# Block 2 of a two-block transformer kernel: the latent values' two parts further apart, and weights behind short pieces split sooner

## The reference

```python
h = rmsnorm(x, pre_norm_mix[l])
proj = h @ w_in[l]
g_a, g_b, qa, ka, va, cq, ckv, kr = jnp.split(proj, SPLIT_IDX, axis=-1)
out_a = swa_sink_alibi_attention(qa, ka, va, positions, sinks[l])
qb = (rmsnorm(cq, q_a_norm[l]) @ w_q_b[l]).reshape(B, S, N_HEADS_B, Q_HEAD_B)
kvb = (rmsnorm(ckv, kv_a_norm[l]) @ w_kv_b[l]).reshape(B, S, N_HEADS_B, KV_HEAD_B)
...
out_b = mla_attention(q_nope, q_rope, k_nope, k_rope, v_b)
merged = jax.nn.sigmoid(g_a) * (out_a @ w_o_a[l]) + jax.nn.sigmoid(g_b) * (out_b @ w_o_b[l])
x = x + rmsnorm(merged @ w_out[l], post_norm_mix[l])
h2 = rmsnorm(x, pre_norm_mlp[l])
y = jnp.square(jax.nn.relu(h2 @ w_up[l])) @ w_down[l]
x = x + rmsnorm(y, post_norm_mlp[l])
```

## Time and profile before

| | us |
|---|---|
| median of three executions | 972.45 |
| lowest, highest | 972.22, 976.34 |
| the profiled execution, its time | 970.76 |
| the profiled execution, span from first to last instruction | 969.5 |
| PE busy | 948.8 (98%) |
| DVE busy | 582.0 (60%) |
| ACT busy | 417.5 (43%) |
| POOL busy | 100.0 (10%) |

### The profile page before, as it was taken

How to read it: one execution, slowest core, us unless ns; L and a number is a source line. 1 busy time by engine, 2 the same in 40 slices (tenths; PEclk the granted TensorE clock), 3 DMA queues, 4 the chain that set the end, 5 groups by cost and what they waited for, 6 DMA issues and landing times.

```text
span 969.5 us, 13623 instructions
## 1 busy us (share of the span) xinstructions
PE 948.8 (98%) x5280; PEld 778.3 (80%) x5280; DVE 582.0 (60%) x1083; ACT 417.5 (43%) x779; POOL 100.0 (10%) x103
## 2 busy tenths in 40 slices
PE   9999999999999998899999999999999999999995
PEld 8778777767898776677778889988888888888895
DVE  6668778687758776665655734863254344334457
ACT  6465265355645254545543235563233133214321
POOL 2005105220220000100002203000000000000020
PEclk9999999999999999999999999999999999999998
DMA  6322111112325211121222352353223322333002
GB/s 243 106 76 76 47 44 66 45 66 77 109 72 183 68 55 52 52 71 55 66 66 88 93 189 88 98 207 109 88 93 103 106 89 87 109 95 100 23 1 87
DMA packets 25806, 85.99 MB, mean 89 GB/s; under 512 B 2960, under 2 KB 5968, under 8 KB 25488
## 3 DMA queue, kind: packets, MB, share of 16 engines
q1 hardware_dynamic: 23952, 79.53, 25.2%
q10 hardware_dynamic: 1552, 5.28, 1.5%
q0 software_dynamic: 240, 0.33, 0.1%
HBM read 80.93 MB, written 4.19 MB: 88 GB/s over the span
## 4 chain that ended last, share of the span: by engine, by line
PE 89%; DVE 7%; ACT 2%; issue 2%; DVEq 0%; ACTq 0%
PE PB L386 13%; PE PB L388 12%; PE PB L387 12%; PE PB L961 5%; PE PB L962 5%; PE PB L960 5%; PE PB L596 4%; PE PB L633 3%; PE PB L611 2%; DVE wl L1439 2%; PE PB L426 2%; PE PB L838 2%; PE PB L840 2%; PE PB L431 1%; PE PB L427 1%
## 5 line engine op out<-in xcount | busy, mean ns | idle before, releaser
L386 PE MATMUL PB<-hh,wh 128*128 128x512 f32 x576 | 238.1, 413 | 2.6 <-DVE X L1943 2.6
L388 PE MATMUL PB<-hh,wl 128*128 128x512 f32 x576 | 225.0, 391 | 0.0
L387 PE MATMUL PB<-hl,wh 128*128 128x512 f32 x576 | 224.6, 390 | 0.0
L1439 DVE TENSOR_TENSOR wl<-raw,wh 128x1024 fp32r<-128x1024 f32 (+2 forms) x90 | 113.9, 1265 | 53.9 <-ACT wh L994 53.9
L386 PEld LDWEIGHTS PB<-hh,wh 128*128 128x128 f32 x576 | 108.2, 188 | 32.0 <-issue 7.3
L387 PEld LDWEIGHTS PB<-hl,wh 128*128 128x128 f32 x576 | 108.4, 188 | 23.9 <-issue 3.4
L388 PEld LDWEIGHTS PB<-hh,wl 128*128 128x128 f32 x576 | 108.1, 188 | 23.3
L994 ACT ACTIVATE wh<-raw 128x1024 fp32r<-128x1024 f32 (+2 forms) x90 | 91.2, 1018 | 49.8 <-PE PB L431 14.0
L1157 ACT ACTIVATE S<-S,sm 128x256 f32<-128x256 f32 (+3 forms) x96 | 50.6, 528 | 120.5 <-DVE sm L1532 94.5
L1439 DVE TENSOR_TENSOR wl<-AR,wh 128x1024 fp32r<-128x1024 f32 x55 | 67.6, 1231 | 43.3 <-ACT wh L994 43.3
L994 ACT ACTIVATE wh<-AR 128x1024 fp32r<-128x1024 f32 x55 | 57.8, 1051 | 70.3 <-PE PB L962 70.3
(11 more groups left out here) (360 smaller groups left out, 1714.4 us busy)
## 6 DMA issues: line engine op xcount, KB each, us to landing
AR<-in_dne SPq DMA_DIRECT2D x32, 512.0 KB, 3.6
AR<-in_upe SPq DMA_DIRECT2D x24, 512.0 KB, 3.5
raw<-in_w2g SPq DMA_DIRECT2D x16, 512.0 KB, 3.5
raw<-in_w1e SPq DMA_DIRECT2D x10, 512.0 KB, 3.5
raw<-in_w1q SPq DMA_DIRECT2D x8, 512.0 KB, 3.4
raw<-in_woab SPq DMA_DIRECT2D x8, 512.0 KB, 3.5
raw<-in_w2e SPq DMA_DIRECT2D x5, 512.0 KB, 4.1
X<-in_xT SPq DMA_DIRECT2D x4, 512.0 KB, 6.5
```

What stands on the lines that cost most here:

```text
L386: e.matmul(bank[:], a[:, col(k)], xa[:, k, :], start=k == 0, stop=False)
L387: e.matmul(bank[:], a[:, col(k)], xb[:, k, :], start=False, stop=False)
L388: i = e.matmul(bank[:], b[:, col(k)], xa[:, k, :], start=False, stop=k == 7)
L1439: e.tensor_tensor(low_, raw_of(c), high.bitcast(F32), ALU.subtract).then_inc(*up("lo", c))
```

## The change

Three tables are made anew. The parts of block 2 from number 8 on lie one beat earlier, except that the second part of the latent values stays at beat 16, so that it has an empty beat before it (before, parts stood at 15 and 16, now at 14 and 16, and the first empty beats 8 and 17 become 15 alone). All later parts are one beat earlier too. `HIGH2` and `LOW2` take the place of the fixed beats `END2[c] - 1` and `END2[c] + 1`: the low part of piece c + 2 is taken at the latest two beats before its first part, and the rounding two beats before that, though not before the product of piece c - 1 has ended.

```diff
 for c in range(CH["w2g", 8], CH["w2g", 7] + 1):
     for part in range({"w2g": 4, "wqr": 2, "wvb": 2, "wqk": 1}[PLAN[c][0]]):
-        t = at * 81 // 72
+        t = at if at < 15 else 16 + (at - 15) * 64 // 57
         FILL2.setdefault(t, []).append((c, part))
         END2[c] = t
         at += 1
+
+FIRST2 = {c: min(t for t, parts in FILL2.items() if any(d == c for d, _ in parts)) for c in END2}
+HIGH2, LOW2 = {}, {}
+for c in sorted(END2):
+    if c + 2 <= max(END2):
+        LOW2[c + 2] = min(END2[c] + 1, FIRST2[c + 2] - 2)
+    else:
+        LOW2[c + 2] = END2[c] + 1
+    HIGH2[c + 2] = max(END2.get(c - 1, 0), min(END2[c] - 1, LOW2[c + 2] - 2))
...
-                for c, end in END2.items():
-                    if t == end - 1:
-                        hi(c + 2)
+                for c, beat_of in HIGH2.items():
+                    if t == beat_of:
+                        hi(c)
...
-                for c, end in END2.items():
-                    if t == end + 1:
-                        lo(c + 2)
+                for c, beat_of in LOW2.items():
+                    if t == beat_of:
+                        lo(c)
```

## The result

| us | before | changed kernel |
|---|---|---|
| median of five executions in one comparison | 975.08 | 966.85 |
| lowest, highest | 972.22, 976.34 | 966.53, 966.97 |
| the profiled execution, its time | 970.76 | 966.85 |
| its span | 969.5 | 965.5 |

The ratio, taken over the executions, is 0.9932 with a 95% interval of 0.9914 to 0.9949: 0.5 to 0.9% faster. It is not the ratio of the two medians, which is 0.9916: the median of five draws from a spread of 4 us moves with the draw, and the two executions that came to the three of the prediction's table, 975.27 and 975.08, raised it from 972.45. Two things stand in this table. The profiled executions differ by 3.9 us, and the sum had said 4.0. But the times of the kernel before reach over 4 us, those of the changed kernel over 0.4, and the median gained more than the profile did. The second fact is what the prediction lacked.

What follows compares the result with a forecast made beforehand. PE bounds the kernel, so only its waits can be saved: 3.4 + 2.85 - 0.9 - 0.7 - 0.25 - 0.3 = 4.1, rounded to 4.0 us, giving 966.8 profiled, 968.4 on the median's scale; range 965.5 to 972.2, own 966.9 to 970.

Steps and rivals of the forecast that it cites:

- the sum: All waits removed and added over the loop: 4.1 us less, rounded down to 4.0 for restarts of the new waits.
- First wait removed: Block 2, before the fourth latent value block: PE's wait for ACT's copy of the first goes, 3.4 us less.
- New wait at the rotation: PE waits 1.1 us for the copy out of PB6, behind piece 52's moved rounding; 0.9 us added.
- The turn of step 3: PE's turn waits for DVE's reading of PB7, getting it at 376.7 for its second half; 0.7 us added.
- Second wait: Before gate piece 54, for DVE to take gate 11: 2.85 us go, about 0.25 stay.
- Step 14's weighted sums: Late in the loop, ACT's gh and query copies precede the copy out of PB6, making PE wait: 0.3 us added.
- The end of the loop: One gate part less before the turn needing step 19's division; 1.4 of 2.9 us cover used, cost nothing.
- the clock: Granted clock was 1.00 in the window with 3.14 us of idle, so no further gain from it: 0.
- (a): Rival: no new waits, ACT and DVE in time; 6.2 us less, 966.2 on the median's scale; chance 0.17.
- (b): Rival: only the first wait goes, the one before piece 54 stays; 1.5 us less, 970.9; chance 0.14.
- (c): Rival: roundings passing copies out of PB6 at eight places cost PE their time; 1.9 us slower, 974.4; chance 0.05.
- (d): Rival: the count of PSUM banks is the bound, waits only move; no change, 972.4; chance 0.04.

Runs made afterwards that it cites:

- `round52`: The changed kernel with the rounding of piece 52 put back behind the gh copy and the copy out of PB6 (beat 13, not 12): median 965.80 us.
- `table_only`: The kernel before with only block 2's parts moved to their new beats, roundings and low parts on the old rule: 967.51 us, ratio 0.994.
- `before_again`: The kernel before with two numbers in a sum swapped, instructions the same: twelve executions from 970.81 to 975.26 us, ratio 0.9999.
- `fill4`: The changed kernel with four unused 128x512 copies added on DVE ahead of taking gate 11: 968.40 to 968.79 us.
- `rule_only`: The kernel before with only the new beats of rounding and low part, block 2's parts left in place: median 970.60 us, ratio 0.9975.
- `fill8`: The changed kernel with eight unused 128x512 copies added on DVE ahead of taking gate 11: one execution at 970.10 us, eleven from 971.79 to 973.03.

## Why the prediction was right, and where it was wrong

**The sum was right.** It gave 966.8 us for a profiled execution; it was 966.85.

- First wait removed, 3.4: the wait is gone. Step 4 was forecast to begin at 373.85 and began at 374.00, and the latent copies were started at 374.69.
- New wait at the rotation, start at 370.6 with 1.1 us of waiting: 370.72 with 1.10. `round52` gives it back, 1.05 for 0.9 in the sum.
- The turn of step 3, second half at 376.7: 376.70. The list shows 0.39 us of waiting; from start to start the turn takes 1.46 us in place of 0.85, so 0.6 for the 0.7 of the sum.
- Second wait, 0.25 left: from the last `wqk` matmul (388.80) to piece 54 (389.21) are 0.41, less 0.23, so 0.2; the turn of step 4 was forecast at 384.8 and came at 384.86.
- Step 14's weighted sums, 0.3: 0.27 of waiting.
- The end of the loop, nothing: no wait there. The 0.27 us that the last window lacks are those of step 14.

The prediction was also right that the rounding of piece 52 makes the new wait at the rotation. But that came with the table and not with the new rule, as `table_only` shows.

**The step that failed is the clock.** The prediction said that from the clock "nothing is to be had", because the granted clock was 1.00 in the window of the long wait. That was true of that one execution, behind the wait too:

```profile
380.00:394.00 14.00, 11.39 (x64) 8.63 (x63) 6.95 (x21) 7.03 (x18) 0.00 (x0) 1.00 0.12 38
```

But of the 78 timed executions of the kernel before only 7 are in the group of 970.7 to 971.1, and that the profile caught one like these was luck. The prediction had the evidence in view: the profiled time, 970.76, lay 1.5 us under the lowest timed one, 972.22, and 1.7 under the median, and I shifted the forecast by this distance without asking where it came from. It is the price of the fallen clock: 1.4 to 1.9 us above 970.7 in 41 of the 78, 2.5 to 3.3 in 11, and 4 to 5.6 in 19. The changed kernel has no wait over 1.10 us in the loop and keeps 0.996 or more in each. So the gain in the median is the 4 us of waiting plus 1.6 to 4.3 us of clock, 5.5 us against 972.4, the median of before in the later comparisons, and 8.2 against the 975.08 of the first. My number, 968.4, should have been the profile's 966.8 for this reason; the wide range of 965.5 to 972.2 held 966.85, the forecast's own range of 966.9 to 970 just missed it. By the number alone rival (a), with 966.2, did better than the forecast: only the profile, with the three new waits in it, tells them apart.

**The chances.** Within half a percent had 0.71, faster by more 0.26. The interval of the ratio lies wholly beyond half a percent. The likeliest class was missed by the clock term alone: the 4.1 us of the sum against 972.4 would be 0.42%.

**The rivals.** (a), no new waits, falls, since all three came. (b), the second wait stays, falls; DVE was done with gate 11 in time. (c), each moved rounding costs PE its time, falls: by the list of waits none of the other seven did, and that of piece 52 cost 1.05 us by `round52`. (d), the banks bound it, falls: with the same three banks the waits are gone. The Trainium skill, "Perfetto Trace Analysis", section "Optimization Strategy", has missing buffers as a reading of repeated gaps; these did not repeat, and here it was the order on ACT and DVE.

The Trainium skill, "TensorE: Matmul & The Clock Gate", section "HAM oscillation — how this bites in real kernels", warns that idle gaps of PE put the next stretch at the lower clock. I had set the neighbouring rule aside on one trace. The runs here agree with it, but in some executions only: the granted clock is 0.50 behind waits of 3.15 and 2.63 us in `before_again` and 1.00 behind the same two, 3.14 and 2.61 us, in the profile of before; behind one of 1.75 us alone it never fell in five executions.

## What to carry to other kernels

Where one engine sets the pace, write down for each of its waits what stands ahead of the releaser on the other engines; durations from one trace then gave the profiled time of this change to 0.1 us, new waits included. It needs each beat and each duration right: one beat read wrongly made the forecast of `table_only` miss by 2.5 us, an assumed copy time that of `fill4` by 1.0. When the timed executions lie above the profiled one, or spread, look at the granted clock of each execution before believing the profile: a wait of some 3 us on TensorE cost its own length and, in some executions only, another 1.5 to 3 us on top; the kernel before has two such waits. Moving work a beat earlier also moves it ahead of something: look for what PE takes from the instruction that was passed.

## What the runs showed of the hardware that was not expected

- The granted clock stays at 0.50 for some us after matmuls have resumed: in `rule_only` PE was busy for all of 380 to 384 us at 0.50, 128x512 matmuls 0.43 us apart in place of 0.23.
- The same program gives distinct times rather than a continuum: 970.7 to 971.1, 972.1 to 972.6, 973.2 to 974.0 and 974.8 to 975.4 us for 77 of 78 executions of the kernel before (one took 976.34). In the profiled one of 975.26 us the clock had fallen twice, for 1.6 and 2.8 us.
- With two waits of 1.73 and 2.61 us, 16 us apart, ten of eleven executions lost the full clock; with one of 2.67 us, 21 us behind one of 1.10, one of six did. Not explained.
- DVE copies of 128x512 from SBUF to SBUF took 0.43 us each in a row (`fill4`, `fill8`), the copy of that size out of PSUM into SBUF 0.69 (PT<-PB in `fill4`).
